# Eight latent steps of a chunked SSD scan: clipped differences per head, swapped PSUM banks, another order of the steps' parts

## What is computed

```python
acum = cumsum(dt * a)                                   # within a chunk
to_end = exp(acum[-1] - acum); chunk_decay = exp(acum[-1])
states = einsum('qn,qr,qrp->rpn', b, to_end * dt, x)    # what the chunk adds to the state
h = h * chunk_decay + states                            # scan over the chunks
cb = einsum('in,jn->ij', c, b)                          # per group
decay = where(i >= j, exp(acum[i] - acum[j]), 0)
y_diag = einsum('ij,ijr,jr,jrp->irp', cb, decay, dt, x)
y_off = einsum('in,rpn,ir->irp', c, h_prev, exp(acum))
y = y_diag + y_off                                      # forward and backward scans are summed
```

## Time and profile before

| | us |
|---|---|
| median of three runs | 4027.34 |
| profiled execution, its own time | 4030.85 |
| span of the profiled execution | 4029.0 |
| the SSD stage in it, first turn to last state update | 673.7 to 902.3 |

### The profile page before, as it was taken

The page is one execution under the profiler, slowest core; times in us unless marked ns, Lnnn a source line. Parts: engine busy times, 40 slices in busy tenths (PEclk is TensorE's granted clock), DMA queues, the critical chain, the costliest instruction groups (busy, mean ns, idle before and its releaser), DMA issues. The chain is left out here.

```text
span 4029.0 us, 44183 instructions
## 1 busy us (share of the span) xinstructions
PE 3579.4 (89%) x17368; PEld 2755.2 (68%) x17368; DVE 1599.8 (40%) x2131; ACT 1419.0 (35%) x1746; POOL 1200.6 (30%) x561
## 2 busy tenths in 40 slices
PE   4989997559976999999828999999999999889999
PEld 1886585447864666666516777777788877768887
DVE  2226533553026666666652333333521232243212
ACT  3215432124223555555323343343432231133222
POOL 0420031443420333333113332322234433133443
PEclk7999998779998999999959999999999998579999
DMA  4312210002222999999733222222132212012222
GB/s 164 110 58 84 84 53 32 0 1 73 94 84 105 332 348 348 353 370 368 296 132 97 71 73 67 70 71 76 37 111 94 97 60 74 1 42 105 96 100 77
DMA packets 94479, 494.55 MB, mean 123 GB/s; under 512 B 21646, under 2 KB 21902, under 8 KB 43760
## 3 DMA queue, kind: packets, MB, share of 16 engines
q1 hardware_dynamic: 74496, 452.75, 31.7%
q0 software_dynamic: 19824, 39.54, 2.7%
HBM read 470.18 MB, written 40.89 MB: 127 GB/s over the span
## 5 line engine op out<-in xcount | busy, mean ns | idle before, releaser
L268 PE MATMUL ps<-arena_r,arena_r 128*128 128x512 f32 x2080 | 846.9, 407 | 41.9 <-POOL ring_r L259 25.0
L269 PE MATMUL ps<-arena_r,arena_r 128*128 128x512 f32 x2080 | 819.1, 394 | 0.0
L259 POOL TENSOR_TENSOR ring_r<-ring,arena_r 128x2048 fp32r<-128x2048 f32 x100 | 464.7, 4649 | 936.3 <-ACT arena_r L255 936.3
L255 ACT ACTIVATE arena_r<-ring 128x2048 fp32r<-128x2048 f32 x166 | 316.7, 1909 | 567.2 <-PE ps L270 411.2
L268 PEld LDWEIGHTS ps<-arena_r,arena_r 128*128 128x128 f32 x2080 | 396.0, 190 | 147.1 <-issue 54.5
L269 PEld LDWEIGHTS ps<-arena_r,arena_r 128*128 128x128 f32 x2080 | 396.4, 191 | 89.5 <-issue 11.2
L259 POOL TENSOR_TENSOR arena_r<-ring,arena_r 128x2048 fp32r<-128x2048 f32 x66 | 304.2, 4609 | 414.2 <-ACT arena_r L255 414.1
L270 PE MATMUL ps<-arena_r,arena_r 128*128 128x512 f32 x1056 | 411.2, 389 | 0.0
L270 PE MATMUL ps<-arena_r,ring_r 128*128 128x512 f32 x1024 | 406.7, 397 | 0.0
L1733 DVE TENSOR_TENSOR arena_r<-arena,arena_r 128x2048 fp32r<-128x2048 f32 x132 | 301.7, 2287 | 170.6 <-ACT arena_r L1691 170.3
L1691 ACT ACTIVATE arena_r<-arena 128x2048 fp32r<-128x2048 f32 x132 | 250.5, 1910 | 127.0 <-DMA arena<-we_gu 104.1
(11 more groups left out here) (374 smaller groups left out, 6185.9 us busy)
## 6 DMA issues: line engine op xcount, KB each, us to landing
ring<-wstream SPq DMA_DIRECT2D x193, 1024.0 KB, 4.9
arena<-we_gu SPq DMA_DIRECT2D x132, 1024.0 KB, 8.1
arena<-we_down SPq DMA_DIRECT2D x66, 1024.0 KB, 7.5
arena<-ys SPq DMA_DIRECT2D x32, 512.0 KB, 9.0
arena<-arena SPq DMA_DIRECT2D x192, 64.0 KB, 2.0
arena<-arena SPq DMA_DIRECT2D x32, 128.0 KB, 4.5
arena<-x_t SPq DMA_DIRECT2D x1, 2048.0 KB, 9.9
h<-arena SPq DMA_DIRECT2D x1, 2048.0 KB, 7.4
```

What stands on the lines that cost most here:

```text
L255: act.activation(whalf(c, 0), ring[:, c % NSLOT, :], ACT.Copy).then_inc(sem("chunk_hi"), 1)
L259: pool.tensor_tensor(whalf(c, 1), ring[:, c % NSLOT, :], whalf(c, 0).bitcast(F32), ALU.subtract).then_inc(sem("chunk_lo"), 1)
L268: pe.matmul(out, hi, rhs[0], start=start, stop=False)
L269: pe.matmul(out, hi, rhs[1], start=False, stop=False)
```

## The change

The step is cut and ordered anew on all four engines.

- DVE: in place of one subtraction (L1034) and one clip (L1038) per half there are eight operations of 128 columns, one for each head, that subtract the head's value and clip in one instruction, straight from PSUM.
- ACT: the exponential of a half's rows now waits for these differences (ssd_seg), and the exponential of the differences is written over the rows after it. B is copied after the four exponentials.
- PSUM: half q of step m lies in banks 4 + 2((m + q) mod 2) and the next one. The outputs of a step are written where its half 0 was; half 0 of the next step goes where this step's half 1 was.
- PE: for a latent step now turns, inner products of the next step, outputs, rows of half 0 of the next step, state matmuls, rows of half 1 of the next step. Only the last waits for ssd_y.
- DVE: state times chunk decay is done ahead of the outputs' addition and goes to a tile of its own (SCALED), from which the state is summed. xdt follows the differences as before.
- POOL: TD of the next step goes ahead of XW.
- The last step of each scan no longer updates its state (NSTATE = 10), as nothing reads it. ACT's part of the next stage's weight chunk waits for the last state, since its place is that of SCALED. The semaphore ssd_sub is gone.

The diff, cut to the lines that are new. Those taken away stand in the functions above; "..." marks where lines are left out:

```diff
@@ -967,42 +967,59 @@
 
             return ap.unsqueeze(2).to_broadcast([P, SSD_H, 64])
 
+        NSTATE = len(STEPS) - 2
+        SCALED = view(R + 32768, 1024)
+
+        def half_bank(m, q):
+
+            return 4 + 2 * ((m + q) % 2)
+
         def ssd_tensor(pe):
...
+            def inner(m):
+                d, t = STEPS[NCTX + m]
                 tok = slice(t * P, t * P + P)
...
+                if m >= 1:
+                    pe.wait_ge(sem("ssd_cb"), m)
+                for g in range(SSD_G):
+                    mm = pe.matmul(bank(3, P, g * P), XBC[:, 8 + g, tok], XBC[:, 12 + g, tok],
+                                   start=True, stop=True)
+                mm.then_inc(sem("ssd_cbmm"), 1)
+
+            def rows(m, q):
+                if q == 0:
                     pe.wait_ge(sem("ssd_tridta"), m + 1)
...
+                elif m >= 1:
+                    pe.wait_ge(sem("ssd_y"), m)
+                for i in range(2):
+                    mm = pe.matmul(bank(half_bank(m, q) + i), C["ones"], TD[:, 8 * q + 4 * i:8 * q + 4 * i + 4, :],
+                                   start=True, stop=True)
+                mm.then_inc(sem("ssd_rows"), 1)
+
+            def turn(n):
+                tok = slice(STEPS[n][1] * P, STEPS[n][1] * P + P)
                 if n >= 1:
...
+                    pe.wait_ge(sem("ssd_state"), min(n, NSTATE))
+                    pe.wait_ge(sem("ssd_btok"), min(n, NSTATE))
                 for j in range(KT):
                     mm = pe.transpose(bank(0, P, j * P), XBC[:, j, tok], C["ident"])
                 mm.then_inc(sem("ssd_xturn"), 1)
...
+                if n < NSTATE:
+                    for g in range(SSD_G):
+                        mm = pe.transpose(bank(2, P, g * P), XBC[:, 8 + g, tok], C["ident"])
+                    mm.then_inc(sem("ssd_bturn"), 1)
+
+            def output(m):
+                d = STEPS[NCTX + m][0]
+                for h in range(SSD_H):
+                    if h % 8 == 0:
+                        pe.wait_ge(sem("ssd_decay"), 2 * m + h // 8 + 1)
+                        pe.wait_ge(sem("ssd_ce"), 2 * m + h // 8 + 1)
+                    o = bank(half_bank(m, 0), P, (h // 2) * P)[64 * (h % 2):64 * (h % 2) + 64, :]
+                    pe.matmul(o, XDT[:, 64 * h:64 * h + 64], DM[:, h, :], start=True, stop=False)
+                    mm = pe.matmul(o, STATE[d][:, 64 * h:64 * h + 64], EC[:, h, :], start=False, stop=True)
+                mm.then_inc(sem("ssd_ymm"), 1)
+
+            def state(n):
                 pe.wait_ge(sem("ssd_xw"), n + 1)
                 pe.wait_ge(sem("ssd_btok"), n + 1)
                 for g in range(SSD_G):
@@ -1010,70 +1027,89 @@
                                    XW[:, g * 256:g * 256 + 256], start=True, stop=True)
                 mm.then_inc(sem("ssd_statemm"), 1)
 
+            for n in range(NCTX):
+                turn(n)
+                state(n)
+            inner(0)
+            for q in range(2):
+                rows(0, q)
+            for n in range(NCTX, len(STEPS)):
+                m = n - NCTX
+                turn(n)
+                if n + 1 < len(STEPS):
+                    inner(m + 1)
+                output(m)
+                if n + 1 < len(STEPS):
+                    rows(m + 1, 0)
+                if n < NSTATE:
+                    state(n)
+                if n + 1 < len(STEPS):
+                    rows(m + 1, 1)
+
         def ssd_vector(dve):
             def xdt(n, d, t):
                 dve.wait_ge(sem("ssd_xturn"), n + 1)
                 if n >= 1:
...
+                    dve.wait_ge(sem("ssd_xw"), min(n, NSTATE))
                 dve.tensor_tensor(split(XDT, SSD_H, 64), split(pf[:, 0:1024], SSD_H, 64), hcol(DT[:, d, t, :]),
                                   ALU.mult).then_inc(sem("ssd_xdt"), 1)
 
             for n, (d, t) in enumerate(STEPS):
...
+                m = n - NCTX
                 if n >= NCTX:
...
                     dve.wait_ge(sem("ssd_cbmm"), m + 1)
                     dve.tensor_tensor(CBM, split(bank(3), SSD_G, P), TRI[d].unsqueeze(1).to_broadcast([P, SSD_G, P]),
                                       ALU.mult).then_inc(sem("ssd_cb"), 1)
...
+                    for q in range(2):
                         dve.wait_ge(sem("ssd_rows"), 2 * m + q + 1)
...
+                        for h in range(8):
+                            ins = dve.tensor_scalar(DM[:, 8 * q + h, :], bank(half_bank(m, q), P, h * P),
+                                                    ACOL[:, d, t, 8 * q + h:8 * q + h + 1], 0.0, ALU.subtract, ALU.min)
+                        ins.then_inc(sem("ssd_seg"), 1)
+                xdt(n, d, t)
+                if n >= NCTX:
                     dve.wait_ge(sem("ssd_cb"), m + 1)
...
+                    for q in range(2):
                         dve.wait_ge(sem("ssd_exp"), 2 * m + q + 1)
...
+                        dve.tensor_tensor(DM[:, 8 * q:8 * q + 8, :].rearrange("p (g r) i -> p g r i", r=4),
+                                          bank(half_bank(m, q), 1024).rearrange("p (g r i) -> p g r i", r=4, i=P),
                                           CBM[:, 2 * q:2 * q + 2, :].unsqueeze(2).to_broadcast([P, 2, 4, P]),
                                           ALU.mult).then_inc(sem("ssd_decay"), 1)
+                if 2 <= n < NSTATE:
+                    dve.wait_ge(sem("ssd_state"), n)
+                    dve.tensor_tensor(split(SCALED, SSD_H, 64), split(STATE[d], SSD_H, 64), hcol(DECAY[:, d, t, :]),
+                                      ALU.mult).then_inc(sem("ssd_decayed"), 1)
+                if n >= NCTX:
                     dve.wait_ge(sem("ssd_ymm"), m + 1)
                     y = Y[:, :, (t - 2) * P:(t - 1) * P]
...
+                    dve.tensor_tensor(y, y, split(bank(half_bank(m, 0), 1024), KT, P), ALU.add).then_inc(sem("ssd_y"), 1)
+                if n < NSTATE:
+                    dve.wait_ge(sem("ssd_statemm"), n + 1)
+                    if n < 2:
+                        dve.tensor_copy(STATE[d], pf[:, 0:1024]).then_inc(sem("ssd_state"), 1)
+                    else:
+                        dve.wait_ge(sem("ssd_decayed"), n - 1)
+                        dve.tensor_tensor(STATE[d], SCALED, pf[:, 0:1024], ALU.add).then_inc(sem("ssd_state"), 1)
 
         def ssd_scalar(act):
...
+            for n in range(len(STEPS)):
+                m = n - NCTX
                 if n >= NCTX:
...
                     if m >= 1:
                         act.wait_ge(sem("ssd_ymm"), m)
                     for q in range(2):
...
+                        act.wait_ge(sem("ssd_seg"), 2 * m + q + 1)
+                        act.activation(EC[:, 8 * q:8 * q + 8, :].rearrange("p h i -> p (h i)"), bank(half_bank(m, q), 1024),
                                        ACT.Exp).then_inc(sem("ssd_erow"), 1)
...
+                        act.wait_ge(sem("ssd_erow"), 2 * m + q + 1)
+                        act.activation(bank(half_bank(m, q), 1024), DM[:, 8 * q:8 * q + 8, :].rearrange("p h i -> p (h i)"),
                                        ACT.Exp).then_inc(sem("ssd_exp"), 1)
+                if n < NSTATE:
+                    act.wait_ge(sem("ssd_bturn"), n + 1)
+                    if n >= 1:
+                        act.wait_ge(sem("ssd_statemm"), n)
+                    act.activation(BTOK, bank(2), ACT.Copy).then_inc(sem("ssd_btok"), 1)
+            act.wait_ge(sem("ssd_state"), NSTATE)
             chunk_hi(act, CH_Z)
 
         def ssd_gpsimd(pool):
@@ -1085,11 +1121,6 @@
                         ec = EC[:, 8 * q:8 * q + 8, :].rearrange("p (g r) i -> p g r i", r=4)
                         cm = XBC[:, 12 + 2 * q:14 + 2 * q, t * P:t * P + P].unsqueeze(2).to_broadcast([P, 2, 4, P])
                         pool.tensor_tensor(ec, ec, cm, ALU.mult).then_inc(sem("ssd_ce"), 1)
...
                 if NCTX <= n + 1 < len(STEPS):
                     dn, tn = STEPS[n + 1]
                     if n >= NCTX:
@@ -1097,6 +1128,12 @@
                     pool.tensor_tensor(TD, TRI[dn].unsqueeze(1).to_broadcast([P, SSD_H, P]),
                                        DTA[:, dn, tn, :].unsqueeze(2).to_broadcast([P, SSD_H, P]),
                                        ALU.mult).then_inc(sem("ssd_tridta"), 1)
+                if n < NSTATE:
+                    pool.wait_ge(sem("ssd_xdt"), n + 1)
+                    if n >= 1:
+                        pool.wait_ge(sem("ssd_statemm"), n)
+                    pool.tensor_tensor(split(XW, SSD_H, 64), split(XDT, SSD_H, 64), hcol(TOEND[:, d, t, :]),
+                                       ALU.mult).then_inc(sem("ssd_xw"), 1)
             chunk_lo(pool, CH_Z)
 
         phases.append(dict(tensor=ssd_tensor, vector=ssd_vector, scalar=ssd_scalar, gpsimd=ssd_gpsimd))
```

More of the change, by code:

```diff
@@ L993, in ssd_tensor @@
                 mm.then_inc(sem("ssd_xturn"), 1)
-                for g in range(SSD_G):
-                    mm = pe.transpose(bank(2, P, g * P), XBC[:, 8 + g, tok], C["ident"])
-                mm.then_inc(sem("ssd_bturn"), 1)
```

(44 more changed lines are left out.)

40 lines of the change are left out of this document (1 added, 39 removed).

## The result

The changed kernel takes 3975.86 us (median of four executions, 3974.42 to 3985.6) against 4026.41 (four executions): 0.988 of the time, 95% interval 0.9862 to 0.9897. By the medians 50.6 us are saved. The forecast was 3982, from 45.1 us saved. The profiled execution took 3985.6 us with a span of 3983.8, that is 45.2 us less than the profiled execution of before.

A forecast was written before the change was run, and what follows sets the result against it. The old step was taken as a 23.8 us chain between engines, the new as PE and DVE's loop of 18.8; with entry and end this saved 45.1 us, 4030.85 to 3985.7, median 3982, range 3973 to 3998.

The forecast's parts named there:

- the first outputs at 721.3: Entry to the SSD latent steps: the first output matmuls start at 721.3 us, where they started at 727.38 before.
- Six steps: Latent steps of the SSD stage: six at 18.8 us each, where a step took 23.8 before, reaching 834.1.
- The last: Last latent step: no state matmuls in front, so 15.2 us, then outputs 6.59 and handoffs with the last y addition 1.3.
- The end: End of the SSD steps: 857.2 us against 902.3 before, with POOL's weight chunk ending near 855.6, hidden.
- The signs on the clock: PE's granted clock in the latent steps: 0.5 to 0.6 in the outputs and 1.00 behind them.
- the starts of the outputs: Output matmuls of successive latent steps: starts 18.4 to 18.9 us apart.
- the rival of the clock staying up: PE's clock stays 1.00 over the gap, outputs take 3.4 us, POOL's 18.43 us loop rules: 3975 us; chance 0.13.
- two loops: One latent step: 18.74 us through PE and DVE, with outputs 6.59, against 18.43 us through POOL; the first taken as longer.
- Part 1: DVE: sixteen small clipped differences at 0.266 us, 4.26 in all, replace 5.54 us a step, gaining 1.3 us.
- the rival in which they don't overlap: DVE's small differences cost 0.35 us each instead of 0.266, adding 10.6 us: 3993 us; chance 0.17.
- Part 4: Triangular rows ahead of XW on POOL; early scaled state leaves 1.1 to 1.7 us of chain, costing POOL 1.08 a step.
- Parts 2 and 3: DVE's 4.17 us idle leaves the chain, ACT's exponentials are covered; reordered PE rows and swapped banks cover y's addition.

The follow-up runs named there:

- a0: The changed kernel run again with no edit: median 3973.0 us, ratio to before 0.9839 to 0.9888, steps 18.26 us.
- e3: Changed kernel with XW ahead of the triangular rows on POOL and state matmuls ahead of half 0's rows on PE: 3966.6 us, step 16.52 us.
- e5: Changed kernel with the next step's inner products done five times, filling PE's gap ahead of the outputs: 3980.6 us, steps 18.27 or 19.8 us.
- e2: Changed kernel without the multiplication of the state by the chunk decay: 3968.9 us, steps 17.3 us, one of 18.2.
- e4: Changed kernel with XW ahead of the triangular rows on POOL alone, PE's order kept: 3988.4 us, steps 19.97 us, two of 21.5.
- e6: Changed kernel with triangular rows halved around POOL's products and XW, state matmuls before rows, mask behind decay products: 3950.6 us, steps 13.99 us, three of 15.3 to 15.7.
- e7: e6 with the next step's inner products done three times, filling PE's gap ahead of the outputs: 3951.2 us, steps 13.99 us.
- e1: Changed kernel with one large difference and one clip per half again instead of eight small operations: 3979.5 us, steps 18.57 us, the first 19.8.
- b1: Kernel before with only the sixteen small clipped differences, all orders as before: 4015.7 us, ratio to before 0.9956 to 0.9984.

## Why the prediction was right

**The sum.** It had the first outputs at 721.3; they started at 722.35, since XW of the last context step was held for 0.9 us by the scaled state (the trace of the changed kernel has L1135 at 2.81 us there), what the text called possible. Six steps were to take 112.8 us and took 109.6. The last was to take 15.2 and took 14.2, and its outputs with the last addition 7.9 and took 6.7. The end was to come at 857.2 and came at 852.8; the stage saved 49.8 us against 45.1. The signs on the clock (0.5 to 0.6 in the outputs) and on the starts of the outputs (18.4 to 18.9 us apart) were missed: 0.57 to 0.71, and 18.2 but for one of 18.4. The median, 3975.9, lies in the range, but at its better end, nearer to the 3975 of the rival of the clock staying up than to the 3982 of the forecast.

**Which chain binds.** This step of the prediction failed. The text worked out two loops, 18.74 us through PE's outputs and 18.43 through POOL, and took the first. It is the second, at 18.25. In a0, e3 and e5 the outputs change by 1 us and more and the step does not; e2, e3 and e4 moved it as POOL's chain says, each to within 0.2 us in the steps whose clock stayed as assumed; and with POOL out of the chain (e6) it fell to 13.99. The term that was too long is the outputs, 6.59 us: they took 5.2 to 5.7 us in six steps and 6.3 to 6.4 in two, at a granted clock of 0.65 to 0.71 and of 0.57 to 0.59, so the first loop was 17.4 to 18.6. In one of these two the loops met, and the distance was 18.36 instead of 18.25. The rival of the clock staying up was half right: it did not stay up, but the step was POOL's, as that rival said. (Its outputs of 3.4 us would be 3.8 by e5 and e7.) That the wrong loop gave nearly the right time is luck: the two sums lay 0.3 us apart.

**Part 1.** The price of a small operation was right: 0.343 us long (forecast 0.35), sixteen in 4.21 to 4.23 (4.26), so the rival in which they don't overlap falls. They start 0.26 us apart, 0.08 less than they last. The Trainium skill (VectorE: DVE Perf Modes, The DRAIN you can't avoid) states that the next operation does not start until the pipe is empty, and, in the same section, that one which is not held starts earlier; these operations agree with the second sentence, which the prediction did not quote. But the gain that the text gave to this part, 1.3 us a step in the new order, was mis-attributed. It subtracted the clips' old durations, 1.6 us, which they had because POOL was in its products. e1 shows them at 0.69 in the new order, but for the one of 2.87. The small operations are worth 13.7 us in the old order (b1), 3.1 to 3.4 in the new one (e1 against the changed kernel), 2.1 of it for that one clip, and the orders alone 43.5: the parts overlap and their gains don't add up.

**Part 4.** The scaled state ran 1.57 us at 741.54 and the triangular rows took 4.59: the 1.0 us that the lock was to cost POOL, and since POOL binds, it costs the step 0.9 (e2). The text counted it in POOL's loop but, having taken the other one, as free. The Trainium skill (SBUF — State Buffer, Who interferes with whom) states that VectorE and GpSimd share a pair of ports as an exclusive lock; e1 agrees both ways: the clip that starts 0.03 us ahead of the product is undisturbed and the product loses 0.5, and the clip that starts 0.03 us behind it waits until it is over.

**Parts 2 and 3.** Both exponentials and y's addition were covered as said: DVE goes from the differences through xdt to both decay products without a pause.

## What to carry to other kernels

Where several engines share a step, write down each engine's loop as a sum of rows before choosing an order, and the difference between the two longest: here it was 0.3 us, and outputs that took about 1 us less than assumed turned it. A duration from a trace is the price of an operation in that order; if it was stretched by a neighbour (here a clip at 1.6 us that is worth 0.69), a change of order gives that back and the cheaper form may gain little. And a short operation on an engine with time to spare can still lengthen the step, if it stops another engine that has none. Where two such operations start at nearly the same time, which of them waits can change from one execution to the next, and with it the time of the whole kernel.

## What had not been expected of the hardware

- Behind a wait of PE of 2.3 to 2.6 us the granted clock fell in some steps and not in others (e4: steps of 19.97 and 21.5; e5: 18.3 and 19.8). Behind waits of 0.9 us (e7, once 1.3) the outputs ran at full clock each time.
- Behind the same idle time of 4.4 us the outputs of the changed kernel started once at full clock (first row 0.45 us) and four times at half (0.70 us); the stretch has 0.57 to 0.72 on the mean either way.
- Two operations of DVE and POOL that start within 0.03 us of each other: one of them stands still until the other is through. It cost 2.1 us once in e1 and, with the work behind it, 7.7 us once in the first trace of the changed kernel.
- The time of the kernel behind the stage varies by 20 us between traces of kernels that are equal there. Such meetings, with the clock lower behind them, are part of it; what makes up the rest was not tried.
